# Four places for fetched weights in the second block, two for what is made of them

## The reference, cut to what matters

```
def squared_relu_mlp(h, w1, w2):
    return jnp.square(jax.nn.relu(h @ w1)) @ w2
...
        if not last:
            ...
            hc2 = rmsnorm(h_ctx, g_pre_ff[l]) * (1.0 + csc2) + csh2
            h_ctx = h_ctx + cg2 * rmsnorm(squared_relu_mlp(hc2, w_ff1[l], w_ff2[l]), g_post_ff[l])
```

## Time and profile before

| | |
|---|---|
| median of three runs | 4224.1 us |
| the profiled execution | 4224.16 us |
| its span, first to last instruction | 4222.2 us |
| PE busy | 3805.4 us, 90% |
| DVE, ACT, POOL busy | 50%, 42%, 41% |
| moved from HBM | 397.32 MB |
| the second block in the trace | from 1307 us to the end |
| the feed-forward part of the context | from 2330 to 2594 us |

### The profile page before, as it was taken

The page is one execution under the profiler, slowest core; times in us unless marked ns, Lnnn a source line. Parts: engine busy times, 40 slices in busy tenths (PEclk is TensorE's granted clock), DMA queues, the critical chain, the costliest instruction groups (busy, mean ns, idle before and its releaser), DMA issues. The chain is left out here.

```text
span 4222.2 us, 61855 instructions
## 1 busy us (share of the span) xinstructions
PE 3805.4 (90%) x22828; PEld 3061.0 (72%) x22828; DVE 2127.8 (50%) x2741; ACT 1753.2 (42%) x2935; POOL 1734.2 (41%) x1158
## 2 busy tenths in 40 slices
PE   4989989999996799877999788999899889999997
PEld 3767767777675687656888777887678668887886
DVE  5536546546445466646324537325666654336224
ACT  3345345354354444445323335324454453334223
POOL 1433434334332422224545566454322234555444
PEclk8999999999998899988999999999999999999999
DMA  6333433433332321112333343333221122332323
GB/s 239 125 113 120 143 105 124 136 114 126 126 102 95 97 70 55 51 45 76 95 94 94 115 135 110 94 95 93 89 70 58 51 65 92 95 95 92 95 95 109
DMA packets 127201, 421.24 MB, mean 100 GB/s; under 512 B 17408, under 2 KB 19088, under 8 KB 126352
## 3 DMA queue, kind: packets, MB, share of 16 engines
q1 hardware_dynamic: 120080, 407.45, 30.2%
q10 hardware_dynamic: 6912, 10.90, 0.8%
HBM read 397.32 MB, written 6.29 MB: 96 GB/s over the span
## 5 line engine op out<-in xcount | busy, mean ns | idle before, releaser
L1785 POOL TENSOR_TENSOR wlo<-wraw,whi 128x512 fp32r<-128x512 f32 x908 | 1268.4, 1420 | 1646.4 <-PE lin L2526 989.7
L1800 ACT ACTIVATE whi<-wraw 128x1024 fp32r<-128x1024 f32 x454 | 476.6, 1058 | 1136.3 <-PE lin L2517 812.1
L2517 PE MATMUL lin<-h_hi,whi 128*128 128x512 f32 (+1 forms) x1856 | 699.1, 384 | 56.2 <-ACT y L2080 14.8
L2517 PE MATMUL lin<-h_lo,whi 128*128 128x512 f32 (+1 forms) x1856 | 686.6, 377 | 0.0
L503 POOL TENSOR_TENSOR wlo<-wraw,whi 128x1024 fp32r<-128x1024 f32 x130 | 319.5, 2458 | 505.0 <-PE lin L1139 356.8
L2517 PE MATMUL lin<-a_hi,whi 128*128 128x512 f32 (+1 forms) x1280 | 480.8, 382 | 30.4 <-ACT tmp L2088 18.1
L2517 PE MATMUL lin<-a_lo,whi 128*128 128x512 f32 (+1 forms) x1280 | 475.9, 378 | 0.0
L2517 PEld LDWEIGHTS lin<-h_hi,whi 128*128 128x128 f32 x1856 | 362.1, 195 | 136.1 <-ACT y L2080 17.7
L2526 PE MATMUL lin<-h_hi,wlo 128*128 128x512 f32 (+1 forms) x1856 | 430.9, 375 | 7.9 <-POOL wlo L1785 7.7
L2517 PEld LDWEIGHTS lin<-h_lo,whi 128*128 128x128 f32 x1856 | 361.9, 195 | 61.6 <-issue 1.5
L2526 PEld LDWEIGHTS lin<-h_hi,wlo 128*128 128x128 f32 x1856 | 327.3, 190 | 72.6 <-POOL wlo L1785 12.3
(11 more groups left out here) (356 smaller groups left out, 6158.3 us busy)
## 6 DMA issues: line engine op xcount, KB each, us to landing
wraw<-in_w SPq DMA_DIRECT2D x544, 512.0 KB, 3.5
mod_ring<-in_w_ada SPq DMA_DIRECT2D x96, 512.0 KB, 4.5
mod_ring<-in_w_mod SPq DMA_DIRECT2D x32, 512.0 KB, 4.5
wraw<-in_dft_tokens SPq DMA_DIRECT2D x32, 512.0 KB, 3.8
turn<-turn SPq DMA_DIRECT2D x144, 64.0 KB, 2.0
first_ring<-in_w_mod SPq DMA_DIRECT2D x16, 512.0 KB, 17.3
tmp<-tmp SPq DMA_DIRECT2D x80, 64.0 KB, 2.0
x<-in_x ACTq DMA_DIRECT2D x2, 2048.0 KB, 21.2
```

The costliest lines, as they stand in the source:

```text
L1785: last = nc.gpsimd.tensor_tensor(wlo[:, s, half], wraw[:, s, half], whi[:, s, half].bitcast(F32), ALU.subtract)
L1800: nc.scalar.activation(whi[:, s, 0:D], wraw[:, s, 0:D], ACT.Copy).then_inc(*w_hi.one)
L2517: last = nc.tensor.matmul(bank[s][:, 0:p.w], whi[:, s, k * P:(k + 1) * P], h[:, k, 0:p.w], start=(k == 0 and h is parts[0]), stop=False)
```

## The change

The fetched weights get four places in the second block: the two of wraw and two of a new tensor late_raw (8 KB in each partition). Chunk g is fetched into place g % 4. whi and wlo keep two places, g % 2. There are four landing semaphores in place of two. SP waits for the remainder of chunk g-4 and not of g-2. ACT waits, before it makes whi of chunk g, for the remainder of chunk g-2 as well; up to now the landing of g implied that, since its load had waited for it. Loops that had a body of two chunks get one of four, on SP, ACT and POOL; PE's and DVE's loops stay. The first block isn't touched.

```diff
+RAW2 = 4
...
-        x, wraw, whi, wlo, cols2 = t["x"], t["wraw"], t["whi"], t["wlo"], t["cols2"]
+        x, whi, wlo, cols2 = t["x"], t["whi"], t["wlo"], t["cols2"]
+        late_raw = sb("late_raw", [P, 2, D])
+        raw_chunk = [(t["wraw"], late_raw)[n // 2][:, n % 2, 0:D] for n in range(RAW2)]
...
-        chunk_in = [Sig(t["raw_in"][s].sem, 8, before // 2 * 16 + 16 - 8 * s) for s in range(2)]
+        chunk_in = [Sig(t["raw_in"][n].sem if n < 2 else sem(f"c_late_in{n}"), 16 // RAW2,
+                        (before // 2 * 16 if n < 2 else 0) + 16 - 16 // RAW2 * n) for n in range(RAW2)]
...
-            def load(g, s, src):
-                sp.wait_ge(*w_split.after(g, -1))
-                sp.dma_start(wraw[:, s, 0:D], src).then_inc(chunk_in[s].sem, 16)
+            def load(g, r, src):
+                sp.wait_ge(*w_split.after(g, 1 - RAW2))
+                sp.dma_start(raw_chunk[r], src).then_inc(chunk_in[r].sem, 16)
...
-                    load(g, g % 2, src)
+                    load(g, g % RAW2, src)
...
-                with sp.Fori(0, n // 2) as i:
-                    for s in range(2):
-                        load(2 * i + (g + s), s, a["w2"][l, bass.ds(2 * i + (at + s), 1)].rearrange("o p n -> p (o n)"))
+                with sp.Fori(0, n // RAW2) as i:
+                    for s in range(RAW2):
+                        load(RAW2 * i + (g + s), (g + s) % RAW2,
+                             a["w2"][l, bass.ds(RAW2 * i + (at + s), 1)].rearrange("o p n -> p (o n)"))
...
-            def split_low(g, s):
+            def split_low(g, r):
+                s = r % 2
                 pool.wait_ge(*w_hi.after(g, 1))
                 pool.wait_ge(*lin_done.after(g, -1))
                 for half in (slice(0, D // 2), slice(D // 2, D)):
-                    last = nc.gpsimd.tensor_tensor(wlo[:, s, half], wraw[:, s, half], whi[:, s, half].bitcast(F32), ALU.subtract)
+                    last = nc.gpsimd.tensor_tensor(wlo[:, s, half], raw_chunk[r][:, half], whi[:, s, half].bitcast(F32), ALU.subtract)
...
-            def split_high(g, s):
+            def split_high(g, r):
+                s = r % 2
+                act.wait_ge(*w_split.after(g, -1))
                 act.wait_ge(*hi_used.after(g, -1))
-                act.wait_ge(*chunk_in[s].after(g, 0))
-                nc.scalar.activation(whi[:, s, 0:D], wraw[:, s, 0:D], ACT.Copy).then_inc(*w_hi.one)
+                act.wait_ge(*chunk_in[r].after(g, 0))
+                nc.scalar.activation(whi[:, s, 0:D], raw_chunk[r], ACT.Copy).then_inc(*w_hi.one)
...
-            def hidden(gi, grp, j, s, w):
-                split_high(gi + 2, s)
+            def hidden(gi, grp, j, r, w):
+                s = r % 2
+                split_high(gi + 2, (r + 2) % RAW2)
...
-                        for s in range(2):
-                            hidden(g + (2 * i + s), q_no + p.ff_no * FF_GROUPS, 2 * i + s, s, p.w)
+                        for n in range(RAW2):
+                            hidden(g + (RAW2 * i + n), q_no + p.ff_no * FF_GROUPS, RAW2 * i + n, (g0 + n) % RAW2, p.w)
```

More of the change, by code:

```diff
@@ L1 @@
 from contextlib import ExitStack
+from functools import partial
 import numpy as np
@@ L1767, in _ @@
             for s in range(2):
-                load(CHUNKS2 + s, s, a["w2"][0, s])
+                load(CHUNKS2 + s, (CHUNKS2 + s) % RAW2, a["w2"][0, s])
             ends = [post_ff(DEPTH - 1, b) for b in range(NB)]
@@ L1784, in split_low @@
                 for half in (slice(0, D // 2), slice(D // 2, D)):
-                    last = nc.gpsimd.tensor_tensor(wlo[:, s, half], wraw[:, s, half], whi[:, s, half].bitcast(F32), ALU.subtract)
+                    last = nc.gpsimd.tensor_tensor(wlo[:, s, half], raw_chunk[r][:, half], whi[:, s, half].bitcast(F32), ALU.subtract)
                 last.then_inc(*w_split.one)
-            with pool.Fori(0, CHUNKS2 // 2) as i:
-                for s in range(2):
-                    split_low(2 * i + (2 + s), s)
+            with pool.Fori(0, CHUNKS2 // RAW2) as i:
+                for n in range(2, RAW2 + 2):
+                    split_low(RAW2 * i + n, n % RAW2)
+            for g in range(CHUNKS2 // RAW2 * RAW2 + 2, CHUNKS2 + 2):
+                split_low(g, g % RAW2)
         @block.scalar
@@ L1921, in refill @@
                     for n in range(1 if c == GV2 + 1 else 2, 3):
-                        split_high(g + n, (g + n) % 2)
+                        split_high(g + n, (g + n) % RAW2)
             def raw(p, c, src):
@@ L2027, in fourier @@
                         for s in range(2):
-                            split_high(g + 2 + s, s)
+                            split_high(g + 2 + s, (g + 2 + s) % RAW2)
                     if h == DFT - 1:
@@ L2098, in outputs @@
                 def outputs(g):
-                    with act.Fori(0, FF_CH // 2) as i:
-                        for s in range(2):
-                            split_high(g + (2 * i + (FF_CH + 2 + s)), s)
+                    with act.Fori(0, FF_CH // RAW2) as i:
+                        for n in range(RAW2):
+                            split_high(g + (RAW2 * i + (FF_CH + 2 + n)), (g0 + FF_CH + 2 + n) % RAW2)
                 act.wait_ge(*lin_free.after(g0, 2))
                 for j in range(FF_CH):
-                    hidden(g0 + j, p.ff_no * FF_GROUPS, j, j % 2, p.w)
+                    hidden(g0 + j, p.ff_no * FF_GROUPS, j, (g0 + j) % RAW2, p.w)
                     if j == 3:
@@ L2119, in feed_forward @@
                 for j in range(FF_CH):
-                    hidden(g + j, grp, j, j % 2, p.w)
+                    hidden(g + j, grp, j, (g0 + j) % RAW2, p.w)
                     if nxt:
@@ L2124, in feed_forward @@
                     gi = g + FF_CH + k
-                    split_high(gi + 2, k % 2)
+                    split_high(gi + 2, (gi + 2) % RAW2)
                     act.wait_ge(*lin_done.after(gi, 1))
```

## The result

| | median us (lowest to highest) | ratio to before (95% interval) |
|---|---|---|
| before | 4223.5 (4216.4 to 4226.3) | 1 |
| changed | 4161.7 (4154.3 to 4166.5) | 0.9855 (0.9836 to 0.9874) |

Each row has four runs; the median of 4224.1 us ahead of the prediction was that of the first three. 62 us less, against 44 forecast. The profiled execution of the changed kernel took 4154.3 us, the fastest of its four; of the 69.8 us between the two spans some 7 are its distance from the median.

The account below looks back on a forecast made before the run. Context chunks were taken as bound by the loop through the weight transfer, 3.79 us per chunk against PE's 2.85. Terms 13.8 + 16.5 + 2 + 6 + 1.5 + 4 = 44 us gave 4224 - 44 = 4180 us, range 4160 to 4207.

Parts of the forecast that it names:

- PE bound throughout: Rival, chance 0.04: DVE in group 4 is slow only because it waits; all eight half groups at 2.85 us per chunk, 4160 us.
- groups 2 and 3, hidden: Context feed-forward: 16 hidden chunks go from 61.3 us to 47.5 at 2.97 each, gain 13.8 us.
- groups 2 and 3, output: Context feed-forward: output chunks at PE's 2.85 us, 0.9 us left of each stall, full clock; 63.9 to 47.4, gain 16.5 us.
- group 1, hidden: Context feed-forward: DVE's residual update sets the pace; only two early pairs can gain, at most 3.3 us, taken as 2.
- group 1, output: Context feed-forward: after PE's wait for a_lo, the way to group 2 falls from 26.8 to 20.8 us, gain 6.0.
- group 4, hidden: Context feed-forward: DVE, adding sums of squares back to back, sets 3.67 us per chunk; 30.92 to 29.4 us, gain 1.5.
- group 4, output: Context feed-forward: DVE normalises the next block without a break there, so gain 0.
- context's projection: Layer 0, twelve narrow chunks: PE's waits for keys (3.59 us) and a query (2.35) shrink; gain 4 us, between 0 and 8.
- Locks: Rival, chance 0.13: POOL and DVE can't overlap in context chunks, so a hidden chunk needs 3.38 us; 4189 us.
- Stall kept: Rival, chance 0.10: at the change from hidden to output chunks the 2.48 us stall and slow clock stay; 4198 us.
- Moved tiles: Slower case, chance 0.03: tiles moved by 8 KB stream slower in 128 latent output chunks, 101 us lost, 4281 us.
- The signs named ahead: Context: no transfer waits, hidden chunks 2.9 to 3.1 us, output half groups about 24, POOL over 85%, idle under 1, no slow clock.

Follow-up runs that it names:

- the first experiment: Changed kernel with one wait put back: SP loads chunk g only after the remainder of chunk g-2, as before; 4216.3 us, ratio 0.9993.
- the square on ACT: Changed kernel with ACT in place of DVE making the unrounded square of the context's hidden rows; 4152.6 us, ratio 0.9846.
- Short adds: Changed kernel with DVE's additions of squares in the context's last hidden chunks on 4 columns in place of 512; 4159.4 us, ratio 0.9853.
- the whole pieces: Changed kernel with POOL's subtraction in one piece of 1024 columns in place of two of 512; 4206.4 us, ratio 0.9967.
- halves: The changed kernel as it is, with POOL's subtraction in two pieces of 512 columns; 4161.7 us, ratio 0.9855.
- the two kernels with quarters everywhere: Changed kernel with POOL's subtraction in four pieces of 256 columns, 4139.7 us; the same with the context's unrounded square on ACT, 4135.4 us.

## Why the prediction was right, and where its sizes were off

The mechanism was right: the loop through the transfer was the bound, it is gone, and the first experiment ties the gain to the start of the load. The gain was 1.4 times what I forecast, and 4161.7 us lies only just inside the range, whose lower end of 4160 I had from a rival (PE bound throughout) whose reason did not hold for group 4: that the range held is in part luck. By its terms, from the profiled executions:

| term | forecast us | measured us |
|---|---|---|
| groups 2 and 3, hidden | 13.8 | 15.2 |
| groups 2 and 3, output | 16.5 | 16.7 |
| group 1, hidden | 2 | 4.4 |
| group 1, output | 6 | 4.9 |
| group 4, hidden | 1.5 | 6.7 |
| group 4, output | 0 | 1.6 |
| context's projection | 4 | 9.0 |
| sum | 44 | 58.5 |

**Groups 2 and 3.** Both terms held. The stall at the change of half groups fell from 0.91 + 2.48 us to one of 0.37, for which I left 0.9:

```profile
2400.97 0.39 PE L2532 MATMUL lin<-a_hi,whi 128*128 128x256 f32 x1 [0.37 <-ACT tmp L2103]
```

The small surplus, 1.4 us, is the hidden chunk: 23.03 / 8 = 2.88 us and not 2.97. My 2.97 was a mean of 3.09 and 2.85, both made of DVE's pieces, and the square on ACT showed that DVE isn't the bound. Its 1.43 us operations were waiting, and it catches up in the next gap.

**Group 4, hidden.** This is the step that failed. I read DVE's back-to-back 3.67 us per chunk as PE's rate. DVE kept that rate after the change:

```profile
2481.55 1.40 DVE L2419 TENSOR_TENSOR tmp<-tmp 128x256 f32<-128x256 f32 x1
2482.98 0.42 DVE L2422 TENSOR_TENSOR a_lo<-tmp,a_hi 128x256 fp32r<-128x256 f32 x1
2483.55 1.56 DVE L2183 TENSOR_TENSOR tmp<-tmp 128x512 f32<-128x512 f32 x1
2485.15 1.41 DVE L2419 TENSOR_TENSOR tmp<-tmp 128x256 f32<-128x256 f32 x1
```

2485.15 - 2481.55 = 3.60 us, yet PE needed 24.3 us for eight chunks, 3.03 each. In the whole half group DVE is busy 19.86 of 24.3 us: the rate holds only for the later chunks. DVE falls behind by 0.7 us in each of these, the two slots between the engines take up part of it, and it is paid once, at the end. There ACT stands behind DVE, and PE behind ACT:

```profile
2496.13 0.63 ACT L1824 ACTIVATE tmp<-x 128x512 f32<-128x512 f32 x1 [1.28 <-DVE tmp L2183]
2496.67 1.04 ACT L1814 ACTIVATE whi<-wraw 128x1024 fp32r<-128x1024 f32 x1
2497.62 0.36 ACT L2103 ACTIVATE tmp<-lin 128x256 f32<-128x256 f32 x1
...
2498.03 0.39 PE L2532 MATMUL lin<-a_hi,whi 128*128 128x256 f32 x1 [2.93 <-ACT tmp L2103]
```

ACT waits 1.28 us for DVE's add, because its own next square needs that slot, and the rounding and the Relu that frees PE's bank stand behind it in ACT's list. 2.93 us idle, and a clock of 0.95 after it. Short adds bring the 2.93 us to 1.74, the square on ACT to 0.69 with the clock at 1.00.

**The projection.** I took one stall of three and no clock. Before, PE also waited 2.19 us at the stage's end:

```profile
1454.21 0.36 PE L2545 MATMUL lin<-h_hi,whi 128*128 128x256 f32 x1 [2.19 <-POOL wlo L1785]
```

After the change this wait and the 2.35 us of the earlier trace rows are gone. Of the 3.59 us there 0.75 stay, and a wait for POOL's remainder of 1.94 us comes up where I had put 1.3:

```profile
1411.52 0.74 PE L2671 MATMUL lin<-whi,h_hi 128*128 128x256 f32 x4 [0.75 <-ACT keys L1909]
1415.63 1.22 PE L2671 MATMUL lin<-wlo,h_hi 128*128 128x256 f32 x8 [1.94 <-POOL wlo L1795]
```

Idle time fell by 5.8 us. The other 3.2 are the clock, which was at half after both stalls of the earlier trace rows (a matmul of 0.58 us) and is 1.00 throughout now. I had priced a stall by its idle time alone.

**Group 1.** 9.3 us in place of 8, with the hidden part above my bound of 3.3: the shares between hidden and output were wrong, their sum nearly right.

**The rest.** The terms that I took as 0 stayed near it: the jumps, the added wait, the first loads and the rotary transfers are together the 0.9993 (0.9983 to 1.0002) of the first experiment, and the latent parts of layer 1 differ by 0.2 us or less. The account by stages isn't closed: 11.3 of the 69.8 us between the profiled executions lie outside the table, 3.6 in the merge of layer 0 and 2.1 in its second latent part. The variant with no earlier load shows 5.8 and 2.5 there, so these don't follow the load.

**The rivals.** Locks: the mechanism is real (the whole pieces show it) but at halves it costs a hidden chunk nothing. Stall kept: fell, 0.37 us. PE bound throughout, 4160 us: nearest in time and right for groups 2 and 3, but not its reason for group 4: of the 21 us that it wanted there 8.3 came, and DVE still holds it. Moved tiles: matmuls of `a_hi` have a mean of 379 ns, 382 before. The signs named ahead came in groups 2 and 3: no wait for a transfer, POOL busy 42.48 + 42.28 of 93.3 us, 91%, output half groups of 23.7 and 23.5 us, clock 1.00. In group 4 one did not: 2.93 us idle before the pair's second bank, and a slow clock behind it. The hidden chunks' 2.88 us lie just under the 2.9 to 3.1 that I gave.

## What to carry to other kernels

Work out the loop of one buffer from rows (load, each engine that reads it, the release), divide by the number of places, and compare with the rate of the engine that should be the bound: 7.58 / 2 = 3.79 against 2.85 said that two places were too few, and one more would do. An engine that is back to back in one stage bounds it only if the stage is longer than the slots between the engines can hide; ask where its lag is paid. And a stall costs more than its idle time: of the 58.5 us here 40.4 were idle time, 8.2 the slow clock after stalls, and about 10 the overlap of matmuls that each pause breaks.

## What the runs showed of the hardware

- A DVE operation with two inputs in SBUF that starts during a POOL operation waits until that one has ended, 0.42 us becoming up to 1.4 with pieces of 512 columns and 2.52 with 1024. Where POOL has work without a break it can wait through about twelve operations of POOL's, 9.13 us; it did so four times in the two kernels with quarters everywhere, while in group 2 of the first of them it waited for one. I had expected quarters to cost the hidden chunks no more than POOL's own 3 us. The total went 4206, 4162, 4140 us from whole over halves to quarters, with the context's hidden chunks slowest at quarters.
- A DVE operation with one input in PSUM is not held up. These rows are of the changed kernel's output chunks of group 2; both of DVE's lie inside POOL's unbroken run:

```profile
2406.92 0.42 DVE L2444 TENSOR_TENSOR y<-lin,y 128x256 f32 x1 [0.54 <-PE lin L2541]
2409.98 0.43 DVE L2444 TENSOR_TENSOR y<-lin,y 128x256 f32 x1 [2.63 <-PE lin L2541]
...
2406.00 5.04 POOL L1795 TENSOR_TENSOR wlo<-late_raw,whi 128x512 fp32r<-128x512 f32 x4 [2.47 <-ACT whi L1814]
```

The same section of the Trainium skill names two inputs in SBUF as a condition, and the trace agrees. It fits that output chunks, which need only this operation, hardly depend on the size of the pieces: group 2 output took 23.7 us with halves, 24.0 with quarters, and 25.3 with one piece, of which 1.46 and 0.50 us are waits at its beginning for what the hidden chunks left late.
